# Row lists for the late expert turns: made turn by turn on the engines, or once through device memory

## The reference

```
scores = sigmoid(tok @ router_w)
sel = scores + router_bias            # only the 4 best of 8 groups of experts remain
top_e = top_k(sel, 8)
wts = scores[top_e] / sum(scores[top_e]) * 2.5
for each block b of 128 rows that belong to one expert e:
    xb = x_pad[rows_of_block]
    hb = silu(xb @ w_gate[e]) * (xb @ w_up[e])
    y[rows_of_block] += (hb @ w_down[e]) * weight_of_row
f = y + shared expert
```

## Time and profile before

| | |
|---|---|
| time, median of 3 runs | 2829.73 us (2825.47 to 2831.87) |
| the profiled execution | 2829.49 us |
| its span in the trace | 2827.7 us |
| TensorE busy | 2677.1 us (95%) |
| VectorE busy | 1870.6 us (66%) |
| ScalarE busy | 1432.4 us (51%) |
| GpSimd busy | 506.9 us (18%) |

### The profile page before, as it was taken

How to read it: one execution, slowest core, us unless ns; L and a number is a source line. 1 busy time by engine, 2 the same in 40 slices (tenths; PEclk the granted TensorE clock), 3 DMA queues, 4 the chain that set the end, 5 groups by cost and what they waited for, 6 DMA issues and landing times. The chain is left out here.

```text
span 2827.7 us, 40561 instructions
## 1 busy us (share of the span) xinstructions
PE 2677.1 (95%) x13972; PEld 1209.8 (43%) x13975; DVE 1870.6 (66%) x3437; ACT 1432.4 (51%) x3340; POOL 506.9 (18%) x404
## 2 busy tenths in 40 slices
PE   7999999999899999999999698997999999999994
PEld 3445666445333433334434264443433334333332
DVE  4996666576667766766765545766676667666655
ACT  1113666243266666666665341322666666666653
POOL 0000000110022222222222211101222222222222
PEclk9999999999999999999999899998999999999998
DMA  9777300201599999999998622016999999998996
GB/s 367 262 271 205 140 16 9 87 31 45 223 343 341 327 305 353 332 369 348 368 325 303 220 90 88 30 53 274 327 300 342 309 376 344 344 372 288 329 323 201
DMA packets 147096, 705.65 MB, mean 250 GB/s; under 512 B 18988, under 2 KB 24364, under 8 KB 94666
## 3 DMA queue, kind: packets, MB, share of 16 engines
q1 hardware_dynamic: 104252, 556.14, 50.4%
q0 software_dynamic: 42336, 144.81, 20.7%
q10 hardware_dynamic: 304, 2.11, 0.2%
HBM read 597.50 MB, written 114.84 MB: 252 GB/s over the span
## 5 line engine op out<-in xcount | busy, mean ns | idle before, releaser
L1700 ACT ACTIVATE xT<-xt_blocks 32x256 f32<-32x256 f32 x2208 | 913.8, 414 | 42.8 <-DVE xt_blocks L1567 15.2
L1779 PE MATMUL exG<-ring,xT 128*32 128x512 f32 (+2 forms) x2352 | 701.3, 598 | 3.5 <-DMA ring<-in_exp_w_up_dram 3.5
L1779 PEld LDWEIGHTS exG<-ring,xT 128*32 128x32 f32 (+2 forms) x2352 | 231.9, 140 | 310.1 <-issue 305.8
L1813 PE MATMUL exD<-ring,ex_hT 128*32 128x512 f32 (+2 forms) x1176 | 355.9, 605 | 2.4 <-DVE w_o L1605 1.2
L1572 DVE TENSOR_SCALAR ex_e<-ex_e 128x256 f32<-128x256 f32 x142 | 44.0, 310 | 429.3 <-ACT ex_e L1712 426.3
L1573 DVE RECIPROCAL ex_e<-ex_e 128x256 f32<-128x256 f32 x142 | 248.9, 1753 | 4.9
L1712 ACT ACTIVATE ex_e<-exG 128x256 f32<-128x256 f32 x142 | 54.5, 384 | 315.0 <-PE exG L1779 315.0
L1779 PE MATMUL exG<-oT,xT 128*32 128x512 f32 (+2 forms) x592 | 197.6, 599 | 1.3 <-DVE xT L1561 1.3
L1779 PE MATMUL exG<-w_fnet,xT 128*32 128x512 f32 (+2 forms) x608 | 176.9, 600 | 1.5 <-DMA ring<-in_exp_w_up_dram 1.5
L1531 DVE TENSOR_TENSOR mod<-place,slots 128x1024 bf16<-128x1024 f32 (+3 forms) x196 | 173.9, 911 | 5.6 <-PEq L234 4.7
L1813 PEld LDWEIGHTS exD<-ring,ex_hT 128*32 128x32 f32 (+2 forms) x1176 | 116.1, 141 | 129.1 <-issue 128.2
(11 more groups left out here) (423 smaller groups left out, 4318.4 us busy)
## 6 DMA issues: line engine op xcount, KB each, us to landing
ring<-in_exp_w_gate_dram SPq DMA_DIRECT2D x64, 1024.0 KB, 10.8
ring<-in_exp_w_up_dram SPq DMA_DIRECT2D x64, 1024.0 KB, 14.8
ring<-in_exp_w_down_dram SPq DMA_DIRECT2D x64, 1024.0 KB, 8.5
ada_w<-in_w_ada_dram SPq DMA_DIRECT2D x48, 512.0 KB, 5.3
oT<-in_exp_w_gate_dram SPq DMA_DIRECT2D x17, 1024.0 KB, 9.7
oT<-in_exp_w_up_dram SPq DMA_DIRECT2D x17, 1024.0 KB, 13.6
oT<-in_exp_w_down_dram SPq DMA_DIRECT2D x17, 1024.0 KB, 8.5
fT<-in_exp_w_gate_dram SPq DMA_DIRECT2D x17, 1024.0 KB, 9.9
```

What stands on the lines that cost most here:

```text
L1700: last = act.activation(xT[m * UNIT:(m + 1) * UNIT, par, :, a * UNIT:(a + 1) * UNIT], parts[a * UNIT:(a + 1) * UNIT, m], ACT.Copy)
L1779: last = pe.matmul(psG[par][p:p + m], xT[:, par, k, p:p + m], ring[s % RING][:, 0:2, k * FF:(k + 1) * FF], start=k == 0, stop=k == KT - 1)
L1813: last = pe.matmul(psD[p:p + m, c], hT[:, k * P + p:k * P + p + m], ring[s % RING][:, 2, k * D + c * 512:k * D + (c + 1) * 512], start=k = ...
```

## The change: what it does

In each layer, the lists of turns 24 to 70 (LIST = 24) are made once, by way of a table in device memory, instead of turn by turn.

- VectorE works out, for each token and each of its eight experts, the line of the table that belongs to it: turn and row. `slot_keys` stands in turn 1, `slot_rows` in turn 2, and `slot_weights`, which writes the weights of a block of 128 tokens into the entries, in turns 3 to 10. All stand between `turn_blocks` and `hidden`.
- GpSimd sends the entries to the table: 64 indirect transfers a layer (`send`), each of 128 entries of 64 bytes, one from each partition. They stand behind the add in turns 4 to 14 (SEND_FROM = 4, SEND_IN = 11), five or six in a turn. In turn 15 it waits for all of them and reads the table back in one transfer of 128 x 1136 float32, 0.58 MB.
- In turn 18 VectorE unpacks it (`slot_lists`) into the lists of rows, targets and weights.
- `onehot`, `index`, `indices` and `targets` are left out for turns 24 to 70. Gathers, adds and weighings of these turns take their columns from the lists. The overflow loop keeps the old way.
- `overflow` goes from turn 9 to turn 17.
- At the kernel's start SP copies a table of empty entries into device memory for each layer (0.58 MB each, ahead of the loads of the conditioning weights). At the start of each expert stage it loads two small constant tables. At the router's end VectorE copies the 512 columns of token weights once more.

```
+            def send(first_entry, last_entry):
+                for c in range(first_entry, last_entry):
+                    t, j = divmod(c, TOP_K)
+                    pool.wait_ge(entries_done, t + 1)
...
+                    pool.indirect_dma_start(out=list_dram[layer].rearrange("p t c -> (p t) c"),
+                                            out_offset=bass.IndirectOffsetOnAxis(ap=slot_at[:, c:c + 1], axis=0),
+                                            in_=entries[:, t, j], in_offset=None).then_inc(listed, 16)
...
             for b in range(1, T):
                 if b + AHEAD <= T:
                     gather(b + AHEAD, (b + AHEAD) % 2, 2)
                 add(b - 1, (b - 1) % 2)
+                i = b - SEND_FROM
+                if 0 <= i < SEND_IN:
+                    send(SENDS * i // SEND_IN, SENDS * (i + 1) // SEND_IN)
+                if i == SEND_IN:
+                    pool.wait_ge(listed, 16 * SENDS)
+                    pool.dma_start(back, list_dram[layer][:, SENDS:].rearrange("p t c -> p (t c)")).then_inc(list_in, 16)
...
+            def slot_keys():
+                dve.wait_ge(caps_in, 16)
+                dve.wait_ge(base_in, 16)
+                wide = lambda a: a.unsqueeze(1).to_broadcast([P, NT, E])
+                list_link(dve.tensor_tensor(part, place[:], wide(caps[:]), ALU.is_lt))
+                list_link(dve.scalar_tensor_tensor(out=part, in0=place[:], scalar=0.0, in1=part, op0=ALU.is_ge, op1=ALU.mult))
+                list_link(dve.tensor_tensor(key, place[:], wide(base), ALU.add))
+                list_link(dve.tensor_tensor(key, key, part, ALU.mult))
...
+            def slot_weights(t):
+                for j in range(TOP_K):
+                    last = dve.scalar_tensor_tensor(out=part[:, j], in0=key[:, t], scalar=slot8[:, t, j:j + 1], in1=wts[:, t],
+                                                    op0=ALU.is_equal, op1=ALU.mult)
...
+            def slot_lists():
+                dve.wait_ge(list_in, 16)
+                dve.wait_ge(half_in, 16)
+                dve.tensor_copy(w_at, lists[:, :, 1]).then_inc(list_ready, 1)
+                dve.tensor_copy(row_at, lists[:, :, 0]).then_inc(list_ready, 1)
...
             for b in range(1, T):
-                if b == 9:
+                if b == 17:
                     overflow()
-                if b + AHEAD < T:
+                if b + AHEAD < LIST:
                     onehot(b + AHEAD, par)
...
                 if b + 2 < T:
                     turn_blocks(b + 2, par)
+                if b == 1:
+                    slot_keys()
+                elif b == 2:
+                    slot_rows()
+                elif b < NT + 3:
+                    slot_weights(b - 3)
+                elif b == LIST - AHEAD - 2:
+                    slot_lists()
                 hidden(b, par, 2)
...
             # TensorE
-                if b + AHEAD < T:
+                if b + AHEAD < LIST:
                     index(b + AHEAD, par)
```

More of the change, by code:

```diff
@@ L60 @@
 TABLE = 256
+SENDS = NT * TOP_K
+ENTRY = 16
 KSLOTS = NT + 2 + CT
@@ L141, in pieces, with list_constants @@
     return [(s, r, p, m) for s, r, _, at, n in turn for p in range(at, at + n, m)]
+def list_constants():
+    f = np.float32
+    p = np.arange(P)
+    base, upper, empty = [], [], []
+    for layer in range(DEPTH):
+        turns, _, _ = schedule(layer)
+        at, half = np.zeros(EXPERTS, f), np.zeros((P, len(turns)), f)
+        for b, turn in enumerate(turns):
+            for i, (_, r, done, row, n) in enumerate(turn):
+                if done == 0:
+                    at[r] = (b + SENDS) * P + row
+                half[row:row + n, b] = i
+        none = np.zeros((P, len(turns), ENTRY), f)
+        none[:, :, 0] = DUMMY + p[:, None]
+        base.append(at)
+        upper.append(half)
+        empty.append(none.reshape(P, -1))
+    return {"list_base": np.stack(base), "list_half": np.stack(upper), "list_empty": np.stack(empty)}
 def constants():
@@ L199, in constants @@
         "caps": np.asarray(UNITS, f) * UNIT,
+        **list_constants(),
     }
@@ L209, in trunk @@
     row_dram = dram("row_scratch", [2, 2 * D])
+    list_dram = [dram(f"list_scratch{l}", [P, SENDS + len(schedule(l)[0]), ENTRY]) for l in range(DEPTH)]
     table_dram = dram("table_scratch", [BLOCKS, 4], I32)
@@ new lines, in slot_rows @@
+                        def slot_rows():
+                            for t in range(NT):
+                                last = dve.max(slot8[:, t], key[:, t])
+                            list_link(last)
+                            keys8 = slot8.rearrange("p t j -> p (t j)")
+                            dve.wait_ge(numbered, 1)
+                            list_link(dve.tensor_tensor(keys8, keys8, nowhere, ALU.max))
+                            list_link(dve.tensor_copy(slot_at, keys8))
+                            list_link(dve.tensor_scalar(slot_at, slot_at, P - 1, None, ALU.bitwise_and))
+                            list_link(dve.tensor_copy(line, slot_at))
+                            dve.tensor_tensor(rank8, keys8, line, ALU.subtract)
+                            list_link(dve.tensor_scalar(line, line, float(SENDS + T), None, ALU.mult))
+                            list_link(dve.scalar_tensor_tensor(out=slot_at, in0=rank8, scalar=1.0 / P, in1=line, op0=ALU.mult, op1=ALU.add))
@@ new lines, in slot_lists @@
+                        def slot_lists():
[3 more added lines that the diff above has]
+                            dve.tensor_copy(row_at, lists[:, :, 0]).then_inc(list_ready, 1)
+                            dve.scalar_tensor_tensor(out=sum_at, in0=lists[:, :, 0], scalar=2.0, in1=half, op0=ALU.mult, op1=ALU.add
+                                                     ).then_inc(list_ready, 1)
```

75 lines of the change are left out of this document (62 added, 13 removed).

## The result

The changed kernel is slower: 2838.05 us in the median of 20 runs against 2826.75, ratio 1.0036 (95% interval 1.0029 to 1.0043). The forecast was 2809. One of its 20 runs, at a lower clock, took 3170.2 us; the ratio leaves it out. The profiled execution has a span of 2838.2 us.

A forecast was written before the change was run, and what follows sets the result against it. TensorE, busy 95% of the span, was taken as the bound. 2829.5 − 21.5 (index groups) + 0.5 (turns 1 and 2) + 0.5 (a send delaying a short turn) = 2809 us; stated range 2800 to 2828, its own range 2804 to 2816.

The forecast's parts named there:

- The gain: Late turns of both layers: 94 index matmul groups leave TensorE at 0.18 to 0.43 us each, saving 21.5 us.
- The forecast's starting point: Profiled execution of the kernel before, 2829.5 us, from which the forecast's terms were taken off or added.
- VectorE's preparation, the fills and the moves: Turns 1 to 10, kernel start and overflow's move: 0.5 us for turns 1 and 2, otherwise taken as 0.
- Cost: 0, up to 1.5 where a turn is short: GpSimd's 64 sends a layer, turns 4 to 14: fit the turn, gather delay mostly free; 0.5 us in the sum.
- the sum of GpSimd's turn: Turns 4 to 14: gather, add, gaps and 5.8 sends at 1.24 us make 10.4 us, fitting into 11.2.
- The rival on sends: Turns 4 to 14: sends exceed GpSimd's turn, gain gone at 1.62 us each, 2861 us at 1.88; chance 0.23.
- a wait of TensorE for one-hots in turns 1 to 14: Sign of error in the preparation turns: TensorE waiting there for one-hots, gathered rows or transposed blocks; no size given.
- The rule weighed there: GpSimd's sends: about 2.0 us fixed cost each, 128 us a layer if GpSimd paid it; judged mostly overlapping completion.
- The rival on transfers: From turn 20 on, weight transfers become the bound and the gain ends at 16 us: 2814 us; chance 0.11.
- if TensorE waits for weights after turn 20: Sign of error in the late turns: TensorE waiting for weights; no size given.

## Why the prediction was wrong

**The gain was right.** Forecast 21.5 us, measured 22.3. (The forecast's starting point, 2829.5, was 2.7 us above the median of 20 runs, which is little beside the miss.) A late place of the earlier trace rows in the changed kernel, gate matmuls followed by 128-row down matmuls, 2.58 us from start to start:

```profile
1501.28 2.74 PE L1919 MATMUL exG<-ring,xT 128*128 128x512 f32 x6
1503.86 3.60 PE L1953 MATMUL exD<-w_o,ex_hT 128*128 128x512 f32 x8
```

**VectorE's preparation, the fills and the moves** were put at 0.5 us in all; the run without sends shows none of it, to within 3 us.

**The step that failed** is "Cost: 0, up to 1.5 where a turn is short", for the sends; it stands in the sum as 0.5 us. Its price for a send was right (1.24 us forecast, 1.26 measured) and so was the sum of GpSimd's turn. What failed is the thought behind it: that a transfer's issue can cost others only by GpSimd's time or the queue's bytes. Plain fills in the sends' place take as much of GpSimd's time and cost the others nothing; the direct transfers have the same bytes, pieces and completions and cost 3 us. At 5.8 indirect sends a turn beside the gather and the add, the sends cost 34 us in this kernel and 28 by themselves. In the traces of those runs, what waits for TensorE goes on up to 8.4 us late, and TensorE's own instructions start in steps of 0.71 us.

**The rival on sends** had the right place and sign and the wrong mechanism: it was to decide at 1.62 us a send, and it decided at 1.26. Of the signs named as proof of error, a wait of TensorE for one-hots in turns 1 to 14 came true, at the end of a chain that began with what followed TensorE's own matmuls late. The rule weighed there, 2.0 us fixed for each transfer (the Trainium skill, page "DMA: Bandwidth & Descriptors", section "Anatomy of one DMA — SWDGE (gpsimd) path"), would have given the right sign through GpSimd's time; the trace shows 1.26 us between sends, so the loss did not come that way.

**The rival on transfers** came true in small, and with it the sign "if TensorE waits for weights after turn 20". Turns 21 to 70 of layer 1 of the changed kernel have 2.4 us of such waits, nearly all in this row; the kernel before has none there:

```profile
PE exG L1919 <- DMA w_fnet<-in_exp_w_up_dram: 2.2, 2, 1.9
```

**What stays open** is where the hold-up sits. That it takes indirect transfers of GpSimd, several in a turn, and not rows, bytes, completions or busy time, is shown. The rows show two forms of it: the engines that wait for TensorE go on late, and TensorE's own instructions start late. As the view models the matmuls' ends, it cannot by itself tell a late signal from a late end. In turn 7 TensorE's weight loads go on mostly 0.43 us apart from 836.84 to 842.64 us, past the matmuls whose signal is still out, which speaks against a late end there. What in an indirect transfer does it is not shown, nor how much of the loss each form makes, nor why two halves in a turn are no better than one run. An indirect transfer with eight index columns at once, which would make 8 sends of 64, was not tried.

## What to carry to other kernels

Count indirect transfers as a resource of their own. In this kernel two in a turn of 11 us (the gather and the add) leave TensorE without a hold-up, five cost some 6 us over the phase, and eight held the whole core up. If a preparation needs many, spread it over as many turns as the list's first use allows; here that turned a loss of 11 us into a gain of 11. Try direct transfers where the places are fixed. And look which wait a removal takes away: once the late turns had no index group, the overflow computation's stall could be put there and vanish, another 13 us.

## What the runs showed of the hardware

While GpSimd issued indirect transfers 1.2 to 1.3 us apart, engines that waited for TensorE went on up to 8.4 us after the end that the view gives its matmuls; in one stall three of them, which waited for different TensorE instructions, went on within 0.14 us. In places TensorE's own instructions came in steps of 0.71 us, with no wait that the profile shows. Fewer rows in a transfer made the loss greater (48 us with 32 rows, 28 with 128). Direct transfers of GpSimd, 0.64 us each, in the same place and with the same pieces, lost 3 us.
